# Seven block products instead of eight in fourteen more pairs of MLP units of a two-block transformer kernel

## The reference

```
m = rms_norm(h, mlp_pre_gain)                     # 256 x 2048
z = square(relu(m @ w_up))                        # w_up   2048 x 8192
z = z @ w_down                                    # w_down 8192 x 2048
h = h + rms_norm(z, mlp_post_gain)
... # second block: attention and merge, then
h2 = rmsnorm(x, g_ffn)
gu = h2 @ w_gu                                    # w_gu 2048 x (2 x 5632)
x = x + (silu(gu[:, :5632]) * gu[:, 5632:]) @ w_down_2
```

## Time and profile before

| | |
|---|---|
| time, median of 3 runs | 2468.47 us (2468.12 to 2468.49) |
| the profiled execution: time, span | 2468.15 us, 2466.3 us |
| busy over the span | PE 2460.2 us, DVE 1609.3 us, ACT 1412.5 us, POOL 67.0 us |
| matmuls | 10957 |
| granted clock of TensorE | 1.000 of full speed |

### The profile page before, as it was taken

One profiled execution on the slowest core, in us unless ns is written; L12 is line 12 of the kernel. 1 busy time (PEld: TensorE's weight loads), 2 busy tenths in 40 slices (PEclk: granted clock), 3 DMA queues, 4 the chain that ended last, 5 costly groups with the idle time before them and its releaser, 6 DMA issues.

```text
span 2466.3 us, 28839 instructions
## 1 busy us (share of the span) xinstructions
PE 2460.2 (100%) x10957; PEld 2038.0 (83%) x10957; DVE 1609.3 (65%) x1743; ACT 1412.5 (57%) x1716; POOL 67.0 (3%) x78
## 2 busy tenths in 40 slices
PE   9999999999999999999999999999999999999999
PEld 8888888888888888888888888888888888888887
DVE  5888576556455565666667645546688667865874
ACT  6886566456455455566576645545655545554553
POOL 0110000000000000010100000000000000000000
PEclk9999999999999999999999999999999999999999
DMA  8997668677677677567756576667766766676665
GB/s 286 264 263 208 205 188 231 206 208 226 199 207 212 196 210 209 160 212 221 228 174 200 184 210 201 200 196 214 240 195 191 230 194 221 182 219 204 217 175 171
DMA packets 348556, 515.34 MB, mean 209 GB/s; under 512 B 113842, under 2 KB 114154, under 8 KB 348170
## 3 DMA queue, kind: packets, MB, share of 16 engines
q1 hardware_dynamic: 343592, 496.63, 66.7%
q0 software_dynamic: 4688, 16.93, 3.1%
q10 hardware_dynamic: 144, 0.01, 0.0%
HBM read 476.52 MB, written 4.47 MB: 195 GB/s over the span
## 4 chain that ended last, share of the span: by engine, by line
PE 98%; DVE 1%; ACT 0%; issue 0%; DMA 0%; POOL 0%; SPq 0%; DVEq 0%; ACTq 0%; POOLq 0%
PE acc L533 26%; PE acc L535 26%; PE acc L534 26%; PE acc L814 4%; PE acc L813 4%; PE acc L815 4%; PE acc L792 1%; PE acc L791 1%; PE acc L793 1%; PE tp L792 0%; PE tp L791 0%; PE tp L793 0%; PE tp L569 0%; PE acc L578 0%; PE po L750 0%
## 5 line engine op out<-in xcount | busy, mean ns | idle before, releaser
L1379 DVE TENSOR_TENSOR w_lo<-raw,w_hi 128x1024 fp32r<-128x1024 f32 x628 | 761.2, 1223 | 540.1 <-ACT w_hi L889 539.6
L889 ACT ACTIVATE w_hi<-raw 128x1024 fp32r<-128x1024 f32 x628 | 659.0, 1058 | 640.5 <-PE acc L535 627.9
L533 PE MATMUL acc<-w_lo,a_hi 128*128 128x512 f32 x1664 | 650.8, 391 | 0.7 <-issue 0.7
L535 PE MATMUL acc<-w_hi,a_lo 128*128 128x512 f32 x1664 | 647.7, 389 | 0.0
L534 PE MATMUL acc<-w_hi,a_hi 128*128 128x512 f32 x1664 | 647.5, 389 | 0.0
L533 PE MATMUL acc<-w_lo,b_hi 128*128 128x512 f32 x1104 | 430.0, 389 | 0.3 <-DVE w_lo L1379 0.3
L534 PE MATMUL acc<-w_hi,b_hi 128*128 128x512 f32 x1104 | 429.5, 389 | 0.0
L535 PE MATMUL acc<-w_hi,b_lo 128*128 128x512 f32 x1104 | 429.5, 389 | 0.0
L1291 ACT ACTIVATE w_hi<-raw 128x1024 fp32r<-128x1024 f32 x220 | 232.5, 1059 | 267.9 <-PE acc L815 135.1
L1971 DVE TENSOR_TENSOR w_lo<-raw,w_hi 128x1024 fp32r<-128x1024 f32 x220 | 268.5, 1224 | 168.2 <-ACT w_hi L1291 166.7
L535 PEld LDWEIGHTS acc<-w_hi,a_lo 128*128 128x128 f32 x1664 | 312.3, 188 | 65.8
(11 more groups left out here) (259 smaller groups left out, 1883.5 us busy)
## 6 DMA issues: line engine op xcount, KB each, us to landing
raw<-w_in_dram SPq DMA_DIRECT2D x272, 512.0 KB, 4.5
raw<-w_down_dram SPq DMA_DIRECT2D x216, 512.0 KB, 4.2
raw<-w_gu_dram SPq DMA_DIRECT2D x136, 512.0 KB, 3.9
raw<-w_up_dram SPq DMA_DIRECT2D x128, 512.0 KB, 4.2
raw<-w_out_dram SPq DMA_DIRECT2D x64, 512.0 KB, 4.2
quad_raw<-w_gu_dram SPq DMA_DIRECT2D x40, 512.0 KB, 4.7
raw<-w_branch_dram SPq DMA_DIRECT2D x32, 512.0 KB, 4.2
tap_sum<-tap_add POOLq DMA_DIRECT2D x20, 512.0 KB, 7.1
```

What stands on the lines that cost most here:

```text
L533: nc.tensor.matmul(out, xh, wl, start=s == 0 and k == 0, stop=False)
L535: mm = nc.tensor.matmul(out, xl, wh, start=False, stop=s == n - 1 and k == KS - 1)
L889: nc.scalar.activation(w_hi[:, ring], raw[:, ring], ACT.Copy).then_inc(hi_ready, 1)
L1379: nc.vector.tensor_tensor(w_lo[:, ring], raw[:, ring], w_hi[:, ring].bitcast(F32), ALU.subtract).then_inc(lo_ready, 1)
```

## The change

Of the sixteen pairs of units of the MLP (two up and two down in each of four blocks), all but the first up pair and the last down pair take the form with seven block products. The loops over MLP blocks become straight code on all engines. The sums of weight blocks and of activations are formed differently (all differences, a fifth buffer `T1`/`T4` in `quad_raw`), and the feed-forward pairs use the same new code. For the up pairs, one set of activation sums (`x_hi`, `x_lo`) is made at the start of the MLP. For the down pairs a set is made once per block, from the unit of z that was joined first (`xd_hi`, `xd_lo`). ACT no longer takes MLP units out of PSUM in these pairs: DVE does so, with the parts added; ACT then rectifies in place (two instructions) and squares (one). DVE adds down units from PSUM straight into `wide`, in two additions per unit (the parts, then `acc`). A transposing transfer now also waits until the unit before has been joined. The buffers take 12 KB more of each partition, and the descriptor memory for transfers issued by POOL is made 4096 bytes.

The slot numbers of a pair count from 0 to 18 in the orders `UP` and `DOWN`; a string is one of the seven products, a pair (unit, slot) a whole slot. In the functions below `g` is the number of the pair's first slot.

```diff
+UP = ("B11", (0, 2), "T2", (0, 3), "T3", (0, 4), "T1", (0, 5), "B21", (0, 6), "T4", (0, 7), "B22",
+      (1, 2), (1, 3), (1, 4), (1, 5), (1, 6), (1, 7))
+DOWN = ("B11", (0, 2), "T2", (0, 3), "T3", (0, 4), "T1", (0, 5), "B21", (1, 2), "T4", (1, 3), "B22",
+        (1, 4), (1, 5), (0, 6), (0, 7), (1, 6), (1, 7))
...
+SUM_AT = {G_PAIR[name] + i: (form, q) for q, name in enumerate(QUADS)
+          for form, i in (("T1", -3), ("T2", 0), ("T3", 1), ("T4", 7))}
...
             def turn_planes(n, stage):
+                if stage == "ff" and n:
+                    sp.wait_ge(join_done, 2 * n)
...
+            def load_block(q, tile, src):
...
+                    g, order = G_PAIR[QUADS[q - 1]], DOWN if QUADS[q - 1][0] == "down" else UP
+                    last = ("T2", "T3", "B21", "B22")[tile]
+                    sp.wait_ge(lo_ready, g + order.index(last) + 1)
+                    sp.wait_ge(quad_sum, 4 * q)
...
+            def load_pair(name, following, turns):
+                blocks = {6: 1, 8: 0, 10: 3, 11: 2}
...
+                for k, (unit, s) in enumerate(steps):
+                    for stage, n in turns.get(k, ()):
+                        turn_planes(n, stage)
+                    load(pair_src(name, unit, s))
+                    if following in QUADS and k in blocks:
+                        tile = blocks[k]
+                        load_block(QUADS.index(following), tile, pair_src(following, tile % 2, tile // 2))
...
+                if (stage, i) == ("up", 1):
+                    turns = {0: [("ff", x)], 6: [("ff", x + 1)]} if b == 0 else {
+                        3: [("ff", x)], 9: [("ff", x + 1)]}
+                if (stage, i) == ("down", 0):
+                    turns = {3: [("ff", x + 2)], 9: [("ff", x + 3)]}
...
# TensorE, in quad_pair
+                    if split0 is not None:
+                        pe.wait_ge(split_lo, split0 + step[1] + 1)
...
# ScalarE
+            def quad_segment(name, tail, own):
...
+                uses(g + 4, g + 5)
+                lead_copied(q)
+                uses(g + 5, g + 6)
+                if behind_quad:
+                    rectify(q - 1, 1)
+                uses(g + 6, g + 7)
+                if behind_quad:
+                    square(b, tail)
+                uses(g + 7, g + 14)
+                if name[0] == "up" and i == 1:
...
+                    nc.scalar.activation(xd_hi[:, :], xd_sum[:, :], ACT.Copy).then_inc(x_hi_ok, 1)
+                uses(g + 14, g + 15)
+                if tail is not None:
+                    join_unit(b, tail)
+                uses(g + 15, g + 16)
+                if tail is not None:
+                    round_unit(b, tail)
+                uses(g + 16, g + 17)
+                if own is not None:
+                    rectify(q, 0)
+                uses(g + 17, g + 18)
+                if own is not None:
+                    square(b, own)
+                uses(g + 18, g + 22)
+                if own is not None:
+                    join_unit(b, own)
+                uses(g + 22, g + 23)
+                if own is not None:
+                    round_unit(b, own)
...
+                        quad_segment(("up", b, i), i or None, 2 * i)
...
+                        quad_segment(("down", b, i), None if i else 3, None)
...
# VectorE
+            def quad_segment(name, early, tail, own):
...
+                uses(g + 4, g + 6)
+                if early is not None:
+                    rows_joined(b, early)
+                uses(g + 6, g + 7)
+                second_sum(q)
+                uses(g + 7, g + 9)
+                third_sum(q)
+                uses(g + 9, g + 10)
+                if tail is not None and (b, tail) != (0, 1):
+                    planes_of(b, tail)
+                uses(g + 10, g + 12)
...
+                    x_sums(b + 1, joined["ff"], xd_sum, (join_done, 2 * (X_MLP + b * NCH + 1)))
+                uses(g + 12, g + 15)
+                if down:
+                    mix(q)
+                uses(g + 15, g + 16)
+                if down:
+                    dve.wait_ge(mixed, q + 1)
+                    wide_add(wide[:, :, 2 * i], parts[:, 0::2]).then_inc(parts_added, 1)
+                else:
+                    dve.wait_ge(z_ready, 4 + b * NCH + own)
+                    unit_evicted(q, 0)
+                uses(g + 16, g + 17)
+                if tail is not None:
+                    rows_joined(b, tail)
+                if down:
+                    wide_add(wide[:, :, 2 * i + 1], parts[:, 1::2]).then_inc(parts_added, 1)
+                uses(g + 17, g + 18)
+                if not down and i == 1:
+                    x_remainders(b + 1, xd_lo, xd_sum, xd_hi)
+                if not down:
+                    mix(q)
+                uses(g + 18, g + 19)
+                if own is not None:
+                    planes_of(b, own)
+                if not down:
+                    uses(g + 19, g + 23)
+                    dve.wait_ge(z_ready, 4 + b * NCH + own)
+                    unit_evicted(q, 1)
+                    return
...
+                        quad_segment(("up", b, i), 0 if i and b else None, i or None, 2 * i)
...
+                        quad_segment(("down", b, i), None if i else 2, None if i else 3, None)
...
-    nc = bacc.Bacc("TRN2", target_bir_lowering=False, num_devices=1)
+    nc = bacc.Bacc("TRN2", target_bir_lowering=False, num_devices=1, dynamic_dma_scratch_size=4096)
```

More of the change, by code:

```diff
@@ new lines, in schedule @@
+def schedule():
+    plan = Schedule()
+    for name, n in (("in", 80), ("out", 32)):
+        plan.begin(name)
+        plan.plain(n)
+    plan.begin("mlp")
+    for b in range(MLP_BLOCKS):
+        for i in range(2):
+            plan.pair_of_units(("up", b, i), None if (b, i) == (0, 0) else UP)
+        for i in range(2):
+            plan.pair_of_units(("down", b, i), None if (b, i) == (MLP_BLOCKS - 1, 1) else DOWN)
+    for name, n in (("qk", 64), ("v", 32), ("g0", 24), ("b0", 8), ("j", 96), ("out2", 32)):
+        plan.begin(name)
+        plan.plain(n)
+    plan.begin("ff")
@@ L84, in feed_forward_slots @@
[L84 to L100, removed]
+            plan.pair_of_units(("ff", b, j), None if (b, j) == (0, 0) else UP)
+        plan.begin(("ff down", b))
+        plan.plain(NCH * FF_SLOTS[b])
@@ L351, in _, with load @@
         def _(sp):
[L352 to L358, removed]
+            loads = [0]
+            def load(src):
+                r = loads[0]
+                if r >= RING:
+                    sp.wait_ge(lo_ready, USE[r - RING] + 1)
+                sp.dma_start(raw[:, r % RING, 0:src.shape[1]], src).then_inc(landed[r % RING], 16)
+                loads[0] += 1
             def ks(s):
@@ new lines, in pair_slot @@
+            def pair_slot(g, unit, s, hi, lo, fresh, last):
+                pe.wait_ge(lo_ready, g + 1)
+                for k in range(KS):
+                    for tk in range(TT):
+                        kt, out = KS * s + k, acc[:, unit, tk, :]
+                        xh, xl = (part[:, kt, tk * P:(tk + 1) * P] for part in (hi, lo))
+                        wh, wl = w_hi[:, g % RING, k, :], w_lo[:, g % RING, k, :]
+                        nc.tensor.matmul(out, xh, wl, start=k == 0 and tk in fresh, stop=False)
+                        nc.tensor.matmul(out, xh, wh, start=False, stop=False)
+                        mm = nc.tensor.matmul(out, xl, wh, start=False,
+                                              stop=last and k == KS - 1)
+                mm.then_inc(slot_used, 1)
@@ L1241, in _ @@
             merge(G_B0, 0, 28, U_B0 % 2)
-            with act.Fori(1, NCH) as j:
+            for j in range(1, NCH):
                 g = G_J - 4 * SPU + j * (4 * SPU)
@@ L1778, in _ @@
             mean_square(4, 38)
-            with dve.Fori(0, NCH) as i:
+            for i in range(NCH):
                 for p_ in range(2):
@@ L1909, in _ @@
             merge(G_B0, U_B0, 0, U_B0 % 2, 0)
-            with dve.Fori(1, NCH) as j:
+            for j in range(1, NCH):
                 g, u = G_J - 4 * SPU + j * (4 * SPU), U_J - 6 + j * 6
```

1012 lines of the change are left out of this document (529 added, 483 removed).

## The result

| | median us | min to max | runs |
|---|---|---|---|
| before | 2468.26 | 2467.85 to 2468.73 | 17 |
| after | 2472.55 | 2468.45 to 2475.28 | 17 |

The ratio is 1.0016, 95% interval 1.0009 to 1.0023: some 4 us slower, just inside the 0.2% that I had called no difference to be told. I had forecast 2454, with a range that ended at 2463. The spread has grown too, from 0.9 us to 6.8. The profiled execution took 2475.28 us and is the slowest of the 17, so its span of 2473.5 us shows the loss at its largest: 7.2 us over before, where the medians are 4.3 us apart.

The account below looks back on a forecast made before the run. PE was taken as the bound, its time being the number of matmuls times their pace. 2468.15 us minus 19.0 for matmuls removed plus 5 of waits gave 2454.1, forecast as 2454, range 2449 to 2463.

Parts of the forecast that it names:

- Matmuls removed: Fourteen MLP pairs lose 6 matmuls each, 84 at 0.2267 us: 19.0 us saved.
- DVE and ACT in a new pair: Both fit in PE's 42.16 us: DVE 38.4 us in the fullest pair, ACT about 34 with two units.
- Table loads and the squares: MLP: no table load expected; squares stay on ACT, since on DVE they would cost 4.6 us at place A.
- place A: Slot 3 of a block's first down pair: w_lo late by 0.5 us with handings-over, four times.
- Place B: Slot 15 of a block's first down pair: fourth unit's rows late by 0.7 us with handings-over, three times.
- I take 4.9: Time in us from SP's issue of a unit's two transposing transfers to ACT's join, taken for all units.
- rival 2: Ways of turned units long throughout, as block loads share the queues: 2457.5 to 2463.5 us, chance 0.18.
- The start and the tail of the MLP: Start: 5 us of DVE sums within 21.8 us; tail: same work in another order, nothing, 1 us either way.
- rival 3: PE waits about a microsecond in every new pair for w_lo behind DVE bursts: 14 us, 2463.5 to 2473, chance 0.06.
- Rival 4: Slower than before: loads become the bound, SP holding loads behind a block load that waits for T4; chance 0.04.
- Rival 1: No wait shows, the way being 4.5 us and handings-over free: 2449.4 to 2451.5 us, chance 0.22.
- My own signs of being wrong: PE waits in up pairs or second down pairs, join's wait over 2 us, or a changed pace in the MLP.

Follow-up runs that it names:

- e4: Changed kernel with the edits of e1, e2 and e3, fourth unit's rows made earlier in down pairs, first new up pair's block loads three steps earlier: 2450.55 us.
- e7: e4 with the squares back on VectorE, ACT only scaling: 2456.50 us.
- e2: Changed kernel with one of a pair's four block loads issued one load later, behind the transposing transfers: 2462.34 us.
- e3: Changed kernel with PE's wait for the activation sums moved from a pair's first step to the first product that reads one: 2469.23 us.
- e1: Changed kernel with PE's wait for unit 1's accumulator in the last, plain down pair moved to just before unit 1's slots: 2466.48 us.
- e5: e4 with the wait for unit 1's accumulator put back where the change has it: 2456.81 us.
- e10: e4 with the first new up pair's block loads back at their old place, three loads later: 2450.71 us.

## Why the prediction was wrong

- **Matmuls removed: right.** 10873, and the pace of 0.2267 us holds wherever PE neither waits nor is throttled. e4 gives 17.7 of the 19.0 us.
- **DVE and ACT in a new pair: right on the average.** DVE is busy 162 us more in the MLP's window (e4, which gets further in it: 184; I said 175, though the terms that I listed for it come to about 162), and the MLP of e4 runs with 684 of 685 us of PE busy. No pair was late for the sum of its work.
- **Table loads and the squares: right.** No load is among ACT's work in the MLP, and e7 bears out the price at place A: 3.6 us of waits there and 6.0 in all, against my 4.6.
- **Place A: right and too large.** I put 0.5 us four times; one wait of 0.6 showed.
- **Place B is a mis-sized term, and the step that failed first.** The place, DVE's part in it and the exception of the last block were right. The term was 0.7 us three times, 2.1; it measured 3.3, 2.5 and 4.5, 10.3 us and the clock besides. What failed is "I take 4.9" for the way of a turned unit, from the issue of its transposes to its join. With the measured ways my own working gives it: the transposes are issued 17.6 us into the pair, a way of 8.16 brings the join at 25.8 where I had 22.9, and 0.7 + 2.9 = 3.6 is late (measured 3.3); with 7.34 it is 0.7 + 2.0 = 2.7 (2.5), with 9.29 it is 0.7 + 4.0 = 4.7 (4.5). I had read the ways from transfers without a block load ahead of them, but the new order puts one directly ahead of this unit's. I had even written in rival 2 that block loads now share the queues, and spread its price over all ways, when it belongs where the order of SP's queue puts one ahead. This working was done behind the result; e2, where the way fell to 5.7 and the waits with it, is its test.
- **The start and the tail of the MLP were put at nothing, and were 3.0 and 3.8 us.** I had counted DVE's work at the start (5 us in 21.8), but neither that DVE would stand idle 4.2 us there for a unit with a way of 8.9 us (I had allowed 6.3 for the first block), nor which of TensorE's waits stands first: the pair waits for all activation sums before its first product, which reads none. At the tail I had called it the same work in another order; there the wait for unit 1's bank stood ahead of unit 0's slots. The order of the waits was to be read in the code. e3 and e1 removed them.
- **What a wait costs was the missing step.** I counted a wait at its length and forecast a full clock. Waits of 3.0 to 4.5 us also lost 8.4 us by the clock, a third of the loss. The clock also goes with the spread of after's runs over 6.8 us: its mean over the execution was 0.998 in the two fastest, 0.997 in fourteen and 0.996 in the slowest (0.001 of the span is 2.5 us), and 1.000 in all five of e4, which spread over 0.7. How much of the spread is the clock and how much the lengths of the waits is open, since one execution alone was profiled.
- **The rivals.** The time fell into rival 3's span, by none of its mechanism: new up pairs after the first show no wait. Rival 2's waits were real, but at the start and at place B and not throughout. Rival 4 did not come: no long wait of TensorE goes back to a plain load. Rival 1 would hold for e4, 2450.55.
- My own signs of being wrong came: PE was not to wait in an up pair or a second down pair and did, at 376.5 and 987.9; the join's wait was to stay under 2 us and was 3.9; and the clock was to stay full.

## What to carry to other kernels

When work is reordered around a transfer, take its time not from the mean of its kind but from what the new order puts ahead of it in the issuing queue; and for each place with little slack ask what stands between the late arrival and its consumer on the engine in the middle, since either of the two alone may be harmless. Read each hand-over wait against the first instruction that needs it: two such waits placed too early cost here 6.1 and 3.3 us (e1, e3), half the gain. A wait of some microseconds of a saturated TensorE is to be priced with the half clock that may follow it. Over all profiles here, the fourteen waits of 2.7 us or more were all followed by it, two of the four of 2.4 to 2.6 us were, and none of 1.1 us or less; in the changed kernel it added 8.4 us to 14.6 us of waits, in e5 2.7 us to a wait of 3.6.

## What the runs showed of the hardware

- Two transposing transfers right behind a plain load and a block load held SP's queue 5.2 to 5.7 us in the changed kernel, and with the block load one load later 3.2 to 3.7 us (e2). For the MLP's first unit it was 6.8 us, 7.6 in e10, and 3.9 with the block loads issued three loads earlier (e4). Where ACT waited for their data, it came 7.3 to 9.6 us after issue in the slow cases (6.0 in e4), and 4.5 us for the units with a hold of 2.6 us.
- Single waits of TensorE, between stretches without a pause, were followed by some microseconds at 1.2 GHz, 427 ns a matmul: behind all of 2.7 us or more, behind one of 2.4 (e1) and one of 2.6 (e3), but not behind one of 2.5 (after) and one of 2.6 (e1). With a wait of 3.8 us filled by matmuls the clock stayed at its upper level, worth 2.7 us.
